# Two FFNs' modulation sums kept as rows, their high half rounded on ScalarE, and a small product before two slabs

## The reference, cut to what matters

```python
def swiglu_ffn(x, w_in, w_out):
    gate, up = jnp.split(x @ w_in, 2, axis=-1)
    return (jax.nn.silu(gate) * up) @ w_out          # width 2816, twice in the first block

# first block: h += 0.5*ffn1(rmsnorm(h)); h += mixer(rmsnorm(h)); h += 0.5*ffn2(rmsnorm(h))
# second block:
c_act = jax.nn.silu(c)                               # [1, 1024]
mod = c_act @ w_ada + b_ada                          # w_ada: [1024, 6144]
shift1, scale1, gate1, shift2, scale2, gate2 = jnp.split(mod, 6, axis=-1)
h = rms_norm(x, g_pre_mix) * (1.0 + scale1) + shift1
```

## Time and profile before

| | |
|---|---|
| median of 3 runs | 1006.28 us |
| profiled execution: time | 1004.26 us |
| its span in the trace | 1002.4 us, mean granted clock 0.991 |
| TensorE busy | 975.8 us (97%), 7645 products |
| VectorE busy | 779.9 us (78%) |
| ScalarE busy | 501.8 us (50%) |
| GpSimd busy | 511.0 us (51%) |
| DMA engines, mean rate | 190 GB/s |

### The profile page before, as it was taken

How to read it: one execution, slowest core, us unless ns; L and a number is a source line. 1 busy time by engine, 2 the same in 40 slices (tenths; PEclk the granted TensorE clock), 3 DMA queues, 4 the chain that set the end, 5 groups by cost and what they waited for, 6 DMA issues and landing times.

```text
span 1002.4 us, 18812 instructions
## 1 busy us (share of the span) xinstructions
PE 975.8 (97%) x7645; PEld 926.8 (92%) x7645; DVE 779.9 (78%) x810; ACT 501.8 (50%) x587; POOL 511.0 (51%) x302
## 2 busy tenths in 40 slices
PE   9999999999989999999999999999989989999997
PEld 8999999998979899999999999978979979999996
DVE  5776565799995679887787779998978887768764
ACT  7433433477541474434334756667657454343432
POOL 4575767610054037577577699999940104314400
PEclk9999999999998999999999999999989999999999
DMA  8966858747360277686776475572236517675641
GB/s 270 360 211 227 275 194 276 242 129 211 96 198 8 84 224 244 232 270 209 261 241 213 140 194 159 142 216 85 85 109 204 193 50 245 228 247 195 216 161 43
DMA packets 166494, 190.06 MB, mean 190 GB/s; under 512 B 10654, under 2 KB 155628, under 8 KB 166316
## 3 DMA queue, kind: packets, MB, share of 16 engines
q1 hardware_dynamic: 165580, 186.13, 57.1%
q0 software_dynamic: 688, 3.07, 1.1%
q10 hardware_dynamic: 176, 0.15, 0.1%
HBM read 187.17 MB, written 2.16 MB: 189 GB/s over the span
## 4 chain that ended last, share of the span: by engine, by line
PE 73%; DVE 15%; POOL 4%; issue 3%; ACT 2%; SPq 1%; DMA 1%; ACTq 0%; DVEq 0%; POOLq 0%
PE ps L2079 46%; PE ps L2123 11%; PE ps L2131 9%; DVE wl L1348 5%; DVE ps L1756 2%; POOL work L825 2%; POOL con L822 2%; PE ps L2364 1%; PE ps L2310 1%; ACT wh L856 1%; PE ps L2175 1%; SPq L564 1%; POOL work L818 1%; PE ps L2151 1%; PE ps L2235 1%
## 5 line engine op out<-in xcount | busy, mean ns | idle before, releaser
L2079 PE MATMUL ps<-xh,wh 128*128 128x256 f32 x1208 | 340.1, 282 | 6.4 <-DVE work L1375 3.2
L2079 PE MATMUL ps<-xl,wh 128*128 128x256 f32 x1208 | 335.4, 278 | 0.0
L2079 PE MATMUL ps<-xh,wl 128*128 128x256 f32 x1208 | 335.2, 278 | 0.0
L1353 DVE TENSOR_TENSOR wl<-raw,wh 128x2048 fp32r<-128x2048 f32 x78 | 231.5, 2968 | 67.4 <-ACT wh L862 67.1
L2079 PEld LDWEIGHTS ps<-xh,wh 128*128 128x128 f32 x1208 | 228.1, 189 | 12.3 <-issue 7.1
L2079 PEld LDWEIGHTS ps<-xl,wh 128*128 128x128 f32 x1208 | 227.8, 189 | 0.5
L2079 PEld LDWEIGHTS ps<-xh,wl 128*128 128x128 f32 x1208 | 227.5, 188 | 0.0
L862 ACT ACTIVATE wh<-raw 128x2048 fp32r<-128x2048 f32 x78 | 149.9, 1922 | 138.3 <-PE ps L2079 101.4
L1348 DVE TENSOR_TENSOR wl<-raw,wh 128x2048 fp32r<-128x2048 f32 (+1 forms) x72 | 181.5, 2527 | 32.7 <-ACT wh L856 32.0
L692 POOL TENSOR_TENSOR ada_raw<-ada_raw,c_act 128x2048 f32<-128x2048 f32 x24 | 90.6, 3775 | 206.5 <-DMA ada_raw<-in_w_ada 201.3
L856 ACT ACTIVATE wh<-raw 128x2048 fp32r<-128x2048 f32 (+1 forms) x74 | 139.5, 1889 | 59.4 <-PE ps L2079 42.3
(11 more groups left out here) (426 smaller groups left out, 1773.0 us busy)
## 6 DMA issues: line engine op xcount, KB each, us to landing
raw<-in_ffn_w_in SPq DMA_DIRECT2D x43, 1024.0 KB, 7.6
ada_raw<-in_w_ada SPq DMA_DIRECT2D x24, 1024.0 KB, 5.1
raw<-in_ffn_w_out SPq DMA_DIRECT2D x22, 1024.0 KB, 6.5
raw<-in_w_in SPq DMA_DIRECT2D x18, 1024.0 KB, 5.3
raw<-in_w_mlp_in SPq DMA_DIRECT2D x16, 1024.0 KB, 5.5
raw<-in_w_mlp_out SPq DMA_DIRECT2D x16, 1024.0 KB, 4.9
raw<-in_w_mix_in SPq DMA_DIRECT2D x14, 1024.0 KB, 5.4
raw<-in_w_mix_out SPq DMA_DIRECT2D x4, 1024.0 KB, 5.2
```

The costliest lines, as they stand in the source:

```text
L1353: dve.tensor_tensor(wl[:, s % SLOTS, :], raw[:, s % SLOTS, :], wh[:, s % SLOTS, :].bitcast(F32), ALU.subtract).then_inc(low_done, 1)
L2079: mm = pe.matmul(bank[:, m * T:(m + 1) * T], w[:, k, m * P:(m + 1) * P], r[:, k, :], start=(m == 0 and k == 0 and j == 0), stop=(k == KT - ...
```

## The change

Within the FFNs' passes GpSimd folds into a buffer of its own (`ada_fold`), so that `ada_raw` is free after the first fold, and SyncE waits for that fold only (`ada_part`, `step * 5 - 3`). ScalarE gets a new step `high_sum` after the SiLU of each pass: it writes the pass's pick matrix (128 x 20, a single column of ones) and rounds the 256 sums to fp32r; GpSimd then subtracts to get the low part. TensorE forms the sum over partitions in one fp32r product per pass: the pick matrix is stationary, high and low parts are the 512 moving columns, and the product accumulates into 20 rows of bank 7, row by row. `long_zeros` after each pass is gone (one stands before ffn1's second slab and clears bank 7), and so is TensorE's wait for the next gate result ahead of it. At the end of ffn2 VectorE copies the 20 rows out and TensorE turns them with four small float32 products (`turn_rows`), in the middle of the last down slab. `few_rows`, a product of 20 stationary and 512 moving columns whose result is overwritten, stands before the second mixer slab and before ffn2's first up slab. The MLP's four pieces keep the old form (`modulation_late`, `modulate_late`). A memset of `qkvp` moves from GpSimd's start to the end of its ffn1 loop.

```diff
 def modulation(step, late=False):            # SyncE
-    if not isinstance(step, int) or step:
+    if late:
         sp.wait_ge(*at("ada_free", step))
+    elif not isinstance(step, int) or step:
+        sp.wait_ge(*at("ada_part", step * 5 - 3))
     sp.dma_start(ada_raw[:, :, :], ...)
 
-def modulation(step):                        # GpSimd, in the FFNs
+def modulation(step, name):
     pool.tensor_tensor(ada_raw, ada_raw, c_act ..., ALU.mult)            # ada_part +1
-    pool.tensor_tensor(flat[:, 0:1024], flat[:, 0:1024], flat[:, 1024:2048], ALU.add)
-    pool.tensor_tensor(flat[:, 0:512], flat[:, 0:512], flat[:, 512:1024], ALU.add)
-    if not isinstance(step, int) or step:
-        pool.wait_ge(*at("ada_taken", step))
-    pool.tensor_tensor(ada_sum[:, :], flat[:, 0:256], flat[:, 256:512], ALU.add).then_inc(S("ada_free"), 1)
+    pool.tensor_tensor(fold[:, :], flat[:, 0:1024], flat[:, 1024:2048], ALU.add).then_inc(S("ada_part"), 1)
+    pool.tensor_tensor(fold[:, 0:512], fold[:, 0:512], fold[:, 512:1024], ALU.add).then_inc(S("ada_part"), 1)
+    pool.tensor_tensor(fold[:, 0:256], fold[:, 0:256], fold[:, 256:512], ALU.add).then_inc(S("ada_part"), 1)
+    pool.wait_ge(*at("ada_part", step * 5 + 5))
+    pool.tensor_tensor(parts[:, 1, :], fold[:, 0:256], parts[:, 0, :].bitcast(F32), ALU.subtract)\
+        .then_inc(S("ada_free"), 1)
 
+def high_sum(step):                          # ScalarE, after silu(i + 2) in each pass
+    if not isinstance(step, int) or step:
+        act.wait_ge(*at("ada_taken", step))
+    act.wait_ge(*at("ada_part", step * 5 + 4))
+    act.activation(step_pick[:, :], step_line[:, bass.ds(step * -1 + (ADA_EARLY - 1), ADA_EARLY)], ACT.Copy)
+    act.activation(ada_parts[name][:, 0, :], ada_fold[name][:, 0:256], ACT.Copy).then_inc(S("ada_part"), 1)
 
-def modulate(step):                          # TensorE
+def modulate(step, name):
     pe.wait_ge(*at("ada_free", step + 1))
-    for m in range(2):
-        mm = pe.matmul(ps[7][:, bass.ds(step * 2 + m, 1)], ada_sum[:, m * P:(m + 1) * P], ones[:, 0:1], start=True, stop=True, ...)
-    mm.then_inc(S("ada_taken"), 1)
+    pe.matmul(ps[7][0:ADA_EARLY, :], step_pick[:, :], ada_parts[name].rearrange("p a t -> p (a t)"), start=False, stop=False, ...)\
+        .then_inc(S("ada_taken"), 1)
 
 def one_pass(i, begin=False):
     ...
-    modulate(i + (0 if name == "ffn1" else FF_STEPS - 1))
-    pe.wait_ge(*at(name + "_gate", i + 2))
-    long_zeros(gate_bank)
+    modulate(i + (0 if name == "ffn1" else FF_STEPS - 1), name)
 
+def few_rows(bank, x):
+    pe.matmul(bank[0:ADA_EARLY, :], x[:, 0, 0:ADA_EARLY], x[:, 0:2, :].rearrange("p a t -> p (a t)"), start=True, stop=True, ...)
 # ffn2:  square_sums(n); ...
+    few_rows(up_bank, high)
     wide(s0 + 1, up_bank, high, low)
 # mixer:
     square_sums("n2")
+    few_rows(ps[5], xh)
 
+def turn_rows():                             # TensorE, in ffn2's last down slab after m == 3
+    pe.wait_ge(*at("ada_rows", 1))
+    for half in range(2):
+        for part in range(2):
+            mm = pe.matmul(ps[7][:, half * ADA_EARLY:(half + 1) * ADA_EARLY],
+                           ada_rows[:, part * T + half * P:part * T + (half + 1) * P], ident[0:ADA_EARLY, 0:ADA_EARLY], ...)
+    mm.then_inc(S("ada_cols"), 1)
 # VectorE, modulation_vectors:
     dve.wait_ge(*at("ada_taken", ADA_EARLY))
+    dve.tensor_copy(ada_rows, ps[7][0:ADA_EARLY, :]).then_inc(S("ada_rows"), 1)
+    dve.wait_ge(*at("ada_cols", 1))
```

More of the change, by code:

```diff
@@ L447, in two_blocks @@
         y_eps, z_eps, scale_m = kr, kr_raw, ps[6][:, T:2 * T]
+        ada_fold = {"ffn1": at_mat, "ffn2": w_v[:, 0:1024]}
+        ada_parts = {"ffn1": yl[:, 0:2, :], "ffn2": xh[:, 4:6, :]}
+        ada_rows = w_kn[0:ADA_EARLY, 0:512]
         gate_row, z_rows, z_junk = w_qn[:, 0:D], w_kn, w_v
@@ L663, in _ @@
                     deep(s + 1 + i * 6, s + 1, "w_mlp_out_2", i * 3 + r)
-                modulation(i + ADA_EARLY)
+                modulation(i + ADA_EARLY, late=True)
             for k in range(ADA_MLP * SLOTS + 1, MLP_STEPS):
@@ L716, in _ @@
             pool.wait_ge(low_done, 3)
-            modulation(0)
+            modulation(0, "ffn1")
             pool.dma_start(con[:, N_CONST_FIRST:N_CONST], a["table"][:, N_CONST_FIRST:]).then_inc(S("con_rest"), 16)
@@ L722, in _ @@
             with pool.Fori(0, FF_STEPS - 2) as i:
-                modulation(i + 1)
+                modulation(i + 1, "ffn1")
+            pool.wait_ge(*at("ada_taken", FF_STEPS - 1))
+            pool.memset(qkvp[:, :, 0:3], 0.0).then_inc(S("pads"), 1)
             def add_pairs(n, ready, src, pairs=range(4)):
@@ L784, in _ @@
             with pool.Fori(0, FF_STEPS - 1) as i:
-                modulation(i + (FF_STEPS - 1))
+                modulation(i + (FF_STEPS - 1), "ffn2")
+            pool.wait_ge(*at("ada_free", ADA_EARLY))
             pool.wait_ge(*at("pos_loaded", 16))
@@ L895, in round_hidden @@
                     act.activation(high[:, :, :], pair(hid[:, 3, :]), ACT.Copy).then_inc(S(name + "_fh"), 1)
+                def high_sum(step):
[4 more added lines that the diff above has]
+                    act.activation(ada_parts[name][:, 0, :], ada_fold[name][:, 0:256], ACT.Copy).then_inc(S("ada_part"), 1)
+                first = 0 if name == "ffn1" else FF_STEPS - 1
                 cast(s0 + 3)
@@ L904, in ffn @@
                     silu(i + 2)
+                    high_sum(i + first)
                     cast_in_loop(s + 4, i, 3, 1)
@@ L912, in ffn @@
                 silu(FF_STEPS)
+                high_sum(first + FF_STEPS - 2)
                 round_hidden(FF_STEPS, last_high[name])
@@ L2151, in long_zeros @@
                 pe.matmul(bank[:, :], zero[0:1, 0:P], zero[0:1, :], start=True, stop=True, skip_group_check=True)
+            def few_rows(bank, x):
+                pe.matmul(bank[0:ADA_EARLY, :], x[:, 0, 0:ADA_EARLY], x[:, 0:2, :].rearrange("p a t -> p (a t)"),
+                          start=True, stop=True, skip_group_check=True)
             def column_sums(n, src, k_tiles, out, ready, signal=True, by_pair=False):
@@ L2169, in one, with modulate_late @@
                 return k + 1
-            def modulate(step):
+            def modulate(step, name):
+                pe.wait_ge(*at("ada_free", step + 1))
+                pe.matmul(ps[7][0:ADA_EARLY, :], step_pick[:, :], ada_parts[name].rearrange("p a t -> p (a t)"), start=False, stop=False, skip_group_check=True)\
+                    .then_inc(S("ada_taken"), 1)
+            def modulate_late(step):
                 pe.wait_ge(*at("ada_free", step + 1))
@@ L2183, in square_sums @@
                 mm.then_inc(S(n + "_stat"), 1)
+            def turn_rows():
[3 more added lines that the diff above has]
+                        mm = pe.matmul(ps[7][:, half * ADA_EARLY:(half + 1) * ADA_EARLY],
+                                       ada_rows[:, part * T + half * P:part * T + (half + 1) * P], ident[0:ADA_EARLY, 0:ADA_EARLY],
+                                       start=(half == 0 and part == 0), stop=(part == 1), skip_group_check=True)
+                mm.then_inc(S("ada_cols"), 1)
             def ffn(name, n, high, low, prev_free):
@@ L2238, in ffn @@
                         mm.then_inc(S(name + "_bank"), 1)
+                    if name == "ffn2" and m == 3:
+                        turn_rows()
                 mm.then_inc(taken, 1)
```

40 lines of the change are left out of this document (29 added, 11 removed).

## The result

The changed kernel is slower. Its median is 1011.89 us in six runs (1006.73 to 1014.43), the kernel before took 1006.12 (1003.28 to 1006.47) beside it; the ratio is 1.0053 (1.0035 to 1.0072). The forecast was 999.8 us, faster, with a range of 990.5 to 1007.0: the sign was wrong and the time lies above the range.

The account below looks back on a forecast made before the run. TensorE's stream of products was taken to bound both FFNs. The terms -12.6 - 1.6 + 7.7 - 1.4 + 1.2 + 0.2 = -6.5 us took the median from 1006.28 to 999.8 us, range 990.5 to 1007.0.

Parts of the forecast that it names:

- Borders: Between FFN passes: one 0.23 us product (bounds 0.11 and 0.46) replaces 0.86 us, saving 12.6 us over 20 passes.
- Ring: In ffn1, loading after the first fold ends TensorE's 0.23 us wait in seven passes, saving 1.6 us.
- Conflict: GpSimd and VectorE exclude each other; seven TensorE waits of 1.1 us at the down slab give back 7.7 us.
- Slower step: After the new waits, TensorE's products can run at the slower step for a slab: 0.2 us lost in all.
- leaves the slower step: Rival: the 20-column product leaves the slower step in 20 passes of 144 products; 1014 us, chance 0.05.
- few_rows: In the mixer and at ffn2's start, 240 + 192 products run at the faster step: net 1.4 us gained.
- Turn: At ffn2's end, four short products and a later bias addition delay the residual update: 1.2 us lost, at most 2.6.

Follow-up runs that it names:

- e7: The kernel before with only GpSimd's folds in a buffer of their own and the early load of `w_ada`: 1002.32 us, ratio 0.9963.
- e4: The changed kernel with `high_sum` one place later in ScalarE's loop, behind the up slab's cast: 1000.14 us, ratio 0.9928.
- e5: The kernel before with the two `few_rows` products and nothing else: 1006.32 us, ratio 1.0013.
- e2: The changed kernel without GpSimd's subtraction and ScalarE's rounding of the sums, the pick waiting for no fold: 995.37 us, ratio 0.9868.
- e1: The changed kernel without the four products that turn the rows, VectorE's copy and the wait between them: 1009.17 us, ratio 1.0014.
- e15: The changed kernel run again, unchanged: 1009.16 us, ratio 1.0043.
- e8: e4 with the turn behind the last down slab and VectorE's bias addition behind the last residual update: 995.87 us, ratio 0.9910.
- e11: e7 with ScalarE also waiting for GpSimd's last fold ahead of its up cast, no work added: 1009.02 us, ratio 1.0028.
- e6: The kernel before without its 20 products of zeros at the border and their wait for the gate result: 1007.45 us, ratio 1.0006.
- e3: The changed kernel with the load of `w_ada` waiting for GpSimd's last operation again: 1035.24 us, ratio 1.0280.
- e10: e8 with the zeros put back behind the 20-row product: 1006.33 us, ratio 0.9990.
- e12: e8 with 100 columns in the pick in place of 20: 998.69 us, ratio 0.9937.
- e13: e8 run again, unchanged: 996.97 us, ratio 0.9925.
- e9: The changed kernel with the zeros and their wait for the gate result put back behind the 20-row product: 1008.52 us, ratio 1.0039.
- e14: e10 run again, unchanged: 1005.19 us, ratio 1.0004.

## Why the prediction was wrong, step by step

- *Borders, -12.6.* Right: 0.23 us from product to slab, free passes of 16.57 us. The bounds 0.11 and 0.46 weren't needed.
- *Ring, -1.6.* Right in kind: e7, which holds this part alone, is faster by 0.37% (0.19 to 0.56), 2 to 6 us; its trace shows the passes at 17.19.
- *Conflict, +7.7: the mechanism was right and the size too small.* Seven waits, every second pass, for the slab subtraction, through `high_sum`'s place: as written. They measured 1.4 us, not 1.1, 10.1 in all. The Trainium skill's page "SBUF — State Buffer" (section "Who interferes with whom") has it that the second of the two engines is blocked. This case's trace agrees, by the 4.09 and 5.48 us above; but in e4, where that goes on, no wait at the down slab comes of it. What I should have priced apart was the order of two lines in ScalarE's loop.
- *Slower step, +0.2: wrong.* I took it from the rows that the faster step follows a 512-column product. At the border it may or may not: 720 products of the passes ran at 0.1178 in the changed kernel's profile, against 144 before (ffn2's first pass, slow before and fast after, belongs to the next term). That is 576 x 0.0044 = 2.5 us more, where I had 0.2. I had tied it to the new waits, and that was wrong as well: e4 has no wait at the down slab and 1152 such products. The rival "leaves the slower step" (1014) was not it either: it wanted all 20 passes.
- *few_rows, -1.4: a third of it came.* ffn2's first 192 products were faster, 0.8 us; the mixer's 240 took 28.28 us again; the two products cost 0.5. That is -0.4. Alone, in e5, the term is worth its 1.4 by the chain.
- *Turn, +1.2: too small.* The end took 4.0 us more, above the bound of 2.6, with the first residual update 4.5 us later than before. Without the hold (e2) it took 2.0 us more; without the turn (e1) the update was still 3.1 us late. The four short products took 1.0 us (0.75 in my sum). The granted clock fell (0.90 over the stretch), which was in no term, but e15 has the late end at 1.00 throughout: the delay of the updates is enough.
- *Not in the sum:* +0.9 us at the start, and some 2 us in the mixer, where the clock falls in any kernel (below).

By the profile: -12.6 - 1.6 + 10.1 - 0.4 + 4.0 + 2.5 + 0.9 + 1.7 (mixer) = +4.6, where the forecast had -6.5; the other 3.7 of the 8.3 us are small gaps behind products and slabs in both FFNs and the mixer's rest, which I didn't trace one by one, so their cause stays open. The steps of the prediction that failed are thus sizes: the conflict (10.1 us for 7.7), the end of ffn2 (4.0 for 1.2), the slower step (2.5 for 0.2), few_rows (0.4 gained for 1.4), and terms that I didn't have. The range failed for that: its upper end took in one term at its bound, not all of them a little over.

The best version with a right result is e8: 0.9910 and 0.9925 of before on two chips, and on the one that ran both 12 us under the changed kernel (996.97 against 1009.16), a little less than I had expected of e15. Its lead over e4 (0.9928) is within the noise of the medians; the profiles show 3.5 us of it at ffn2's end.

## What to carry to other kernels

When an in-order engine gets a new instruction that waits for a slow engine, put it behind everything that the critical engine needs of it, and price the hold apart from the work: here 0.6 us of work a pass cost 9 us in the profiles' passes, and 11 to 12 between the medians, by its place. The hold by itself isn't the price either: in longer passes with one operation less (e11) the trace has a single wait of 1.0 us. Two engines that lengthen each other do little harm as long as nobody on the path queues behind the slower one. And where a step of the bottleneck takes two lengths, count how many passes are at each before crediting an instruction with either.

## What the hardware showed that I had not expected

A 256-column product follows the one before at 0.1134 or 0.1178 us, with the granted clock at 1.00 in both. The step can hold over hundreds of products and over equal borders (nine slow passes of ffn2 in e6, nine fast ones in the kernel before). All 39 changes to the slower step between neighbouring slabs of the passes, in the 17 profiles, come with a gap: the slab's second product starts at least 0.16 us after its first, where an unbroken stream has 0.11 or 0.12. But not every gap brings one, and the way back needs none, as in e8, where slow down products, the 20-row product and fast gate products follow each other:

```profile
71.54 5.65 PE ps L2181 x48
77.19 0.24 PE ps L2237
77.43 10.88 PE ps L2137 x96
```

What it will be after a border I can't say. That is open.

In the mixer, the stretch from the slab at 287 to the one at 319 us took one of three lengths: 28.4 us in eight profiles (e1, e3, e4, e7, e8, e10, e12 and e13), 31.2 or 31.3 in before, e2, e5, e6, e9, e11 and e15, 32.9 in the changed kernel and e14. Short products with waits between them go before it; what differs is when and for how long the granted clock is at 1.2 GHz. In the shortest it falls once, near the start, in the middle ones there and again some 13 us later, in the longest once, 12 us in, and for longer. Windows of ten microseconds, before, the changed kernel and e4, which is 3.6 us further on in its work (the third column from the end is the granted clock):

```profile
300.00:310.00 10.00, 10.00 (x62) 10.00 (x62) 4.67 (x7) 0.60 (x1) 9.66 (x8) 0.66 0.13 42
```

```profile
300.00:310.00 10.00, 10.00 (x49) 10.00 (x48) 3.31 (x7) 0.17 (x1) 9.66 (x8) 0.50 0.15 52
```

```profile
300.00:310.00 10.00, 9.95 (x88) 9.68 (x87) 6.80 (x10) 1.71 (x3) 8.53 (x6) 1.00 0.00 0
```

Up to 4.5 us of a run hang on this, in kernels that are alike there; of the 8.3 us between the two profiles 1.7 lie here. Behind the first GLU slab the kernels are alike too, and their profiles take 440 to 445 us. A difference of a few us between two profiles is an effect of the change only where the stretch shows it.
